# Turned projections: x's hi and lo parts in one 512-column product, copies in eight places, and an addition of halves

## The reference

```python
def first_block(x, ...):
    for l in range(DEPTH):                                   # 2
        x = x + 0.5 * swiglu_ffn(rms_norm(x, ffn1_norm[l]), ffn1_w1[l], ffn1_w2[l])
        h = rms_norm(x, mix_norm[l])
        gm_u, gm_v, r_q, r_k, r_v, r_g, n_q, n_kv, n_g = jnp.split(h @ w_in[l], splits, axis=-1)
        y_a = gmlp_mixer(gelu(gm_u), gelu(gm_v), ...)
        y_b = retention_mixer(r_q, r_k, r_v, r_g, ...)
        y_c = nsa_mixer(n_q, n_kv, n_g, ...)                 # compressed keys, then attention
        g_a, g_b, g_c = jnp.split(sigmoid(h @ w_merge_gate[l] + b_merge_gate[l]), 3, axis=-1)
        mix = g_a * (y_a @ w_branch_out[l, 0]) + g_b * (y_b @ w_branch_out[l, 1]) + g_c * (y_c @ w_branch_out[l, 2])
        x = x + mix @ w_o[l]
        x = x + 0.5 * swiglu_ffn(rms_norm(x, ffn2_norm[l]), ffn2_w1[l], ffn2_w2[l])

def second_block(x, ...):
    for layer in range(DEPTH):                               # 2
        proj = rms_norm_2(x, norm_mix_g[layer]) @ w_in[layer]
        (a_in, bq, bk, bv, cq, ck, cv, co, cgate, dq, dk, dv, gates) = split_cols(proj)
        ys = [fourier_mix(a_in), gqa_branch(bq, bk, bv, ...), mlstm_branch(cq, ck, cv, co, cgate, ...),
              diff_branch(dq, dk, dv, ...)]
        merged = sum(sigmoid(gates[n]) * (ys[n] @ w_branch[layer][n]) for n in range(4))
        x = x + merged @ w_out[layer]
        x = x + conv_ffn(rms_norm_2(x, norm_ffn_g[layer]), ...)
```

## Time and profile before

| | |
|---|---|
| median of 3 runs | 2251.74 us (2251.03 to 2252.18) |
| the profiled execution's own time | 2251.06 us |
| its span in the profile | 2249.3 us |
| instructions | 30453 |
| TensorE matmuls | 12350, busy 2228.1 us |
| VectorE busy | 1532.7 us |
| ScalarE busy | 1209.2 us |
| weight loads | 368 of 1024 KB, median 4.8 us to landing |

### The profile page before, as it was taken

One profiled execution on the slowest core, in us unless ns is written; L12 is line 12 of the kernel. 1 busy time (PEld: TensorE's weight loads), 2 busy tenths in 40 slices (PEclk: granted clock), 3 DMA queues, 4 the chain that ended last, 5 costly groups with the idle time before them and its releaser, 6 DMA issues.

```text
span 2249.3 us, 30453 instructions
## 1 busy us (share of the span) xinstructions
PE 2228.1 (99%) x12350; PEld 1897.9 (84%) x12350; DVE 1532.7 (68%) x2116; ACT 1209.2 (54%) x1808; POOL 65.8 (3%) x118
## 2 busy tenths in 40 slices
PE   8999999999999999999999999999999999999998
PEld 7888987888888889878888888888888888888887
DVE  6567578665665576786566856786777766776766
ACT  6456455554554564555555655455556555455554
POOL 0000000000000000000000100000000100000000
PEclk9999999999999999999999999999999999999999
DMA  8565553455545645434655534444554444445553
GB/s 285 191 231 187 205 183 137 169 189 195 192 175 194 239 176 205 180 138 172 243 187 188 187 132 169 150 159 185 189 188 177 179 150 161 157 162 184 188 187 113
DMA packets 62804, 409.38 MB, mean 182 GB/s; under 512 B 7977, under 2 KB 9513, under 8 KB 15305
## 3 DMA queue, kind: packets, MB, share of 16 engines
q1 hardware_dynamic: 62664, 407.44, 49.8%
HBM read 405.83 MB, written 2.10 MB: 181 GB/s over the span
## 4 chain that ended last, share of the span: by engine, by line
PE 92%; DVE 4%; ACT 2%; DMA 1%; POOL 1%; issue 1%; SPq 0%; POOLq 0%; DVEq 0%; ACTq 0%
PE bank L584 19%; PE bank L585 19%; PE bank L586 19%; PE bank L631 18%; PE bank L638 9%; DVE w_lo L270 2%; DMA w_raw<-in_tiles 1%; PE bank L393 1%; PE bank L1721 1%; PE bank L1733 1%; PE bank L2332 0%; PE bank L1876 0%; PE bank L2500 0%; PE bank L2039 0%; PE bank L2049 0%
## 5 line engine op out<-in xcount | busy, mean ns | idle before, releaser
L270 DVE TENSOR_TENSOR w_lo<-w_raw,w_hi 128x2048 fp32r<-128x2048 f32 x367 | 835.1, 2283 | 56.5 <-ACT w_hi L240 56.1
L240 ACT ACTIVATE w_hi<-w_raw 128x2048 fp32r<-128x2048 f32 x359 | 684.9, 1911 | 107.0 <-DMA w_raw<-in_tiles 106.6
L631 PE MATMUL bank<-hT,w_hi 128*128 128x512 f32 x1920 | 459.7, 391 | 0.7 <-DVE w_lo L270 0.7
L631 PEld LDWEIGHTS bank<-hT,w_hi 128*128 128x128 f32 x1920 | 355.6, 188 | 72.7 <-DVE w_lo L270 1.5
L584 PE MATMUL bank<-w_hi,hT 128*128 128x512 f32 (+2 forms) x832 | 327.5, 394 | 1.3 <-DVE w_lo L223 1.3
L586 PE MATMUL bank<-w_hi,hT 128*128 128x512 f32 (+2 forms) x832 | 318.5, 383 | 0.0
L585 PE MATMUL bank<-w_lo,hT 128*128 128x512 f32 (+2 forms) x832 | 318.3, 383 | 0.0
L638 PEld LDWEIGHTS bank<-hT,w_lo 128*128 128x128 f32 x1920 | 247.7, 191 | 10.3
L638 PE MATMUL bank<-hT,w_lo 128*128 128x256 f32 x1920 | 250.9, 283 | 0.0
L584 PEld LDWEIGHTS bank<-w_hi,hT 128*128 128x128 f32 x832 | 156.6, 188 | 38.2 <-issue 7.8
L586 PEld LDWEIGHTS bank<-w_hi,hT 128*128 128x128 f32 x832 | 156.3, 188 | 31.2
(11 more groups left out here) (395 smaller groups left out, 2987.0 us busy)
## 6 DMA issues: line engine op xcount, KB each, us to landing
w_raw<-in_tiles SPq DMA_DIRECT2D x368, 1024.0 KB, 4.8
a_cmp_w<-in_cmp_w SPq DMA_DIRECT2D x2, 2048.0 KB, 7.7
shifted<-in_bias SPq DMA_DIRECT2D x12, 256.0 KB, 6.6
w_raw<-in_tiles SPq DMA_DIRECT2D x8, 256.0 KB, 5.6
a_gm_rows<-in_rows SPq DMA_DIRECT2D x2, 768.0 KB, 7.1
x_res<-in_x SPq DMA_DIRECT2D x2, 512.0 KB, 5.0
a_ret_rows<-in_rows SPq DMA_DIRECT2D x2, 512.0 KB, 8.3
b_rows<-in_rows SPq DMA_DIRECT2D x2, 512.0 KB, 5.9
```

The lines of the kernel that those rows point to most:

```text
L240: act.activation(k.hi[slot][:], k.raw[slot][:], ACT.Copy).then_inc(k.hi_done[slot], 1)
L270: dve.tensor_tensor(k.lo[slot][:], k.raw[slot][:], k.hi[slot][:].bitcast(F32), ALU.subtract).then_inc(k.lo_done[slot], 1)
L631: pe.matmul(bank[:], k.hi[slot][:, w], k.hT[:, c].rearrange("p a s -> p (a s)"), start=c == 0, stop=False)
```

## The change

A new role `"B"` takes the place of `"T"` for six tiles of block 1 (rqT, rkT, kcvcT, two of nqT, kskwT) and for all ten turned tiles of block 2: 32 tiles over the two layers of each. The two tiles of uT, which go through a Gelu, stay.

For a B unit TensorE runs `both_parts` (8 matmuls of 512 columns) and `lo_part` (8 of 256) into a bank of its own: each unit is now a group, not each tile. ScalarE copies each unit's whole bank (L1141) into one of eight places in the buffers `gate` and `mix`, and VectorE adds the two halves into the output (L1185); a copy waits for the addition eight earlier. `proj_out` of such a tile is now the addition. TensorE signals twice per tile. `Gqa.rope` handles the units of `gqa_a1` before the fold. Waits on other tiles' outputs are added where a mixer begins.

```diff
-            self.units += [(n0, h, h == 1, group, role) for h in range(2)]
-            group += 1
+            apart = role[0] == "B"
+            self.units += [(n0, h, h == 1, group + h * apart, role) for h in range(2)]
+            group += 1 + apart
...
+        self.parts = [a[:].rearrange("p a b -> p (a b)")[:, 2 * SEQ * i:2 * SEQ * (i + 1)] for i in range(4)
+                      for a in (gate, mix)]
...
+            elif role[0] == "B":
+                self.copies += 1
+                key = "act"
+                counts[key] += 1
+                counts["taken"] += 1
+                self.copy_at[u] = self.copies, counts[key]
+                self.proj_out[n] = (self.taken, self.copies)
...
-        first = role[-1] == 0 if role[0] in ("wide", "wgate") else half == 0 or role[0] == "wbranch"
+        first = role[-1] == 0 if role[0] in ("wide", "wgate") else half == 0 or role[0] in ("wbranch", "B")
...
+        elif role[0] == "B":
+            both_parts(pe, k, slot, half, bank)
+            lo_part(pe, k, slot, half, bank).then_inc(k.used[slot], 1)
...
+        if role[0] == "B":
+            copy, _ = self.copy_at[u]
+            k.ring.wait_used(act, n, half + 1)
+            if copy > 8:
+                act.wait_ge(self.taken, copy - 8)
+            act.activation(self.parts[copy % 8], self.bank(group)[:], ACT.Copy, scale=role[1][1]).then_inc(self.act_out, 1)
...
+        if role[0] == "B":
+            copy, at = self.copy_at[u]
+            part = self.parts[copy % 8]
+            dve.wait_ge(self.act_out, at)
+            dve.tensor_tensor(role[2][:, half], part[:, 0:SEQ], part[:, SEQ:2 * SEQ], ALU.add).then_inc(self.taken, 1)
...
         link(last)
+        f.vector(dve, "gqa_a1", lo=False)
         self.fourier.fold(dve)
```

More of the change, by code:

```diff
@@ L39 @@
 WIDE1 = (0, 6, 8, 14)
+BOTH1 = (4, 5, 10, 11, 12, 13)
 F1_AT = 0
@@ L1006, in __init__ @@
         self.tmp = ph.sb("f_tmp", [P, 2, SEQ])
+        self.parts = [a[:].rearrange("p a b -> p (a b)")[:, 2 * SEQ * i:2 * SEQ * (i + 1)] for i in range(4)
+                      for a in (gate, mix)]
+        self.copy_at, self.copies = {}, 0
         self.biased = None if bias is None else ph.sem("f_biased")
@@ L1039, in partial @@
             return role[-1] == 0
-        return not last_half and role[0] != "wbranch"
+        return not last_half and role[0] not in ("wbranch", "B")
     def bank(self, group):
@@ L1117, in activate @@
         n, half, last_half, group, role = self.units[u]
-        if role[0] == "wgate":
+        if role[0] == "B":
[4 more added lines that the diff above has]
+            act.activation(self.parts[copy % 8], self.bank(group)[:], ACT.Copy, scale=role[1][1]).then_inc(self.act_out, 1)
+        elif role[0] == "wgate":
             b, c, kh = role[1:]
+            if kh and not b and self.copies:
+                act.wait_ge(self.taken, self.copies)
             gate = self.gate[:, half, c * 512:(c + 1) * 512]
@@ L1154, in combine @@
         n, half, last_half, group, role = self.units[u]
-        if role[0] == "wgate":
+        if role[0] == "B":
[3 more added lines that the diff above has]
+            dve.tensor_tensor(role[2][:, half], part[:, 0:SEQ], part[:, SEQ:2 * SEQ], ALU.add).then_inc(self.taken, 1)
+        elif role[0] == "wgate":
             b, c, kh = role[1:]
             if kh and self.bias is not None:
+                if not b:
+                    dve.wait_ge(self.taken, self.copies)
                 k.ring.wait_used(dve, n, half + 1)
@@ L2660, in __init__ @@
             ("T", G, uT[:, 0:2], "act"), ("T", G, uT[:, 2:4], "act"),
-            ("T", C, rqT[:], "act"), ("T", C, rkT[:], "act"),
+            ("B", C, rqT[:], "act"), ("B", C, rkT[:], "act"),
             ("wide", C, rv, "act"), ("wide", S, rg, "act"),
-            ("T", C, kcvcT[:], "act"), ("T", Q, nqT[:, 0:2], "act"), ("T", Q, nqT[:, 2:4], "act"),
-            ("T", C, kskwT[:], "act"), ("wide", None, Columns((vsvw, *C), (gates, *T)), "act")],
+            ("B", C, kcvcT[:], "act"), ("B", Q, nqT[:, 0:2], "act"), ("B", Q, nqT[:, 2:4], "act"),
+            ("B", C, kskwT[:], "act"), ("wide", None, Columns((vsvw, *C), (gates, *T)), "act")],
             BRANCHES1, self.bias, gate, mix, ys)
@@ L2731, in __init__ @@
             ("wide", C, qkv[:, :, 0:512], "act"), ("wide", None, Columns((qkv[:, :, 512:768], *C), (g16, *C)), "act"),
[L2732 to L2734 removed]
+            ("B", C, aT[:, 0:2], "act"), ("B", C, aT[:, 2:4], "act"),
+            ("B", C, cqT[:, 0:2], "act"), ("B", C, cqT[:, 2:4], "act"),
+            ("B", C, ckT[:, 0:2], "act"), ("B", C, ckT[:, 2:4], "act"),
             ("wide", C, va[:, :, :, 0:P], "act"), ("wide", T, og, "act"),
[L2736 to L2737 removed]
+            ("B", C, dqT[:, 0:2], "act"), ("B", C, dqT[:, 2:4], "act"),
+            ("B", C, dkT[:, 0:2], "act"), ("B", C, dkT[:, 2:4], "act"),
             ("wide", C, dv, "act")],
@@ L2789, in pool, with middle_signals @@
         self.diff.pool(pool)
-def middle_signals(proj_tiles, wide_at, branches):
-    return [2 if n - 1 in wide_at else 1 for n in range(proj_tiles)] + [2] * (branches * MERGE_TILES) + [1] * (OUT_TILES - 1) + [2]
+def middle_signals(proj_tiles, wide_at, both_at, branches):
+    return [2 if n - 1 in wide_at or n in both_at else 1 for n in range(proj_tiles)] + [2] * (branches * MERGE_TILES) + [1] * (OUT_TILES - 1) + [2]
 def windows(shifted):
@@ L2828, in program @@
             at1.append((ring.add(ffn_places(base + F1_AT), FFN_SIGNALS),
-                        ring.add(list(range(base + PROJ1_AT, base + F2_AT)), middle_signals(PROJ1_TILES, WIDE1, BRANCHES1)),
+                        ring.add(list(range(base + PROJ1_AT, base + F2_AT)), middle_signals(PROJ1_TILES, WIDE1, BOTH1, BRANCHES1)),
                         ring.add(ffn_places(base + F2_AT), END_SIGNALS if l == DEPTH - 1 else FFN_SIGNALS)))
@@ L2832, in program @@
             base = BLOCK2_AT + l * STREAM2
-            at2.append((ring.add(list(range(base + PROJ2_AT, base + UP_AT)), middle_signals(PROJ2_TILES, WIDE2, BRANCHES2)),
+            at2.append((ring.add(list(range(base + PROJ2_AT, base + UP_AT)), middle_signals(PROJ2_TILES, WIDE2, BOTH2, BRANCHES2)),
                         ring.add(ffn_places(base + UP_AT), END_SIGNALS if l == DEPTH - 1 else FFN_SIGNALS)))
```

4 lines of the change are left out of this document (added).

## The result

| | before | changed |
|---|---|---|
| median | 2251.47 us (20 runs, 2248.96 to 2253.12) | 2256.60 us (20 runs, 2253.53 to 2258.52) |
| the profiled execution's own time | 2251.06 us | 2257.90 us |
| its span | 2249.3 us | 2256.2 us |

The ratio is 1.0021, 95% interval 1.0015 to 1.0027. The change costs 5.1 us, 0.23%: slower, as forecast, but by less than half of the +11.8 us of the sum. The two profiled executions lie 6.84 us apart, since the one of the changed kernel is among its slower ones; terms are compared with this 6.84.

A forecast was written before the change was run, and what follows sets the result against it. TensorE, busy 2228.1 of 2249.3 us, was taken to bound the kernel. Merging -7.0, nqT waits +4.9 and +3.2, rv +1.0, Fourier +4.7, clock +5.0 gave +11.8, so 2263.5 us; range 2255.5 to 2269.5.

The forecast's parts named there:

- the sum: Whole kernel: savings of merging plus new waits and clock falls, +11.8 us, giving 2263.5 us; chance 0.55.
- merging, 32 tiles: Turned projections of both blocks: 16 of 48 matmuls go, saving 0.22 us a tile, -7.0 us.
- wait at nqT: Block 1: third nqT unit waits for ScalarE's first copy, behind tile 14's conversion; 4.9 us layer 1, 3.2 layer 2.
- rv's first matmul: Block 1: it waits for ScalarE's copy of rkT's first unit, delayed behind VectorE's work; 0.5 us per layer, +1.0.
- Fourier stretch: Block 2, before the Fourier copy: four VectorE additions cost 1.45 us, four tiles' savings lost; 2.33 per layer, +4.7.
- clock: Behind the longer waits in blocks 1 and 2: three more falls to 1.2 GHz, +5.0 us; bounds none and twice that.
- the fixed cost of a matmul: TensorE: the skill's about 2.5 ns per matmul would give back 1.3 us for 512; the prediction took 12 ns from rows.
- merging buys nothing: Turned projections: fewer matmuls give no gain, so the 7.0 us are gone; from rows +17.0, 2268.7 us; chance 0.03.
- What costs nothing: Elsewhere: extra ScalarE copies (19 us), VectorE additions (27 us), signals and added waits don't delay TensorE; 0 us.
- the late one named there: Block 1: VectorE's retention chain comes 1.8 us later, covered by the nqT wait; without that, some 1.3 us.
- the rival in which the waits come and the clock doesn't fall more: Both blocks: the new waits appear without further clock falls; +6.8 us, 2258.5 us; chance 0.22 for waits with fewer falls.

The follow-up runs named there:

- The two experiments on GpSimd: pool_free_before and pool_held_after, which move VectorE's `w_lo` away from or back beside GpSimd's root operation in block 2: 2252.78 and 2262.30 us.
- pool_free_before: Kernel before, with block 2's VectorE `w_lo` beside GpSimd's root moved behind the scaling of the heads: 2252.78 us, ratio 1.0002.
- pool_held_after: Changed kernel, with that block 2 `w_lo` put ahead of aT's first two additions, beside GpSimd's root again: 2262.30 us, ratio 1.0043.
- best: Changed kernel, tile 14's load before kcvcT's transfers, block 1's `w_lo` before additions, block 2's `w_lo` behind Fourier copies: 2240.97 us, ratio 0.9950.
- before_fm: Kernel before, with only block 2's `w_lo` in front of the Fourier copies made behind them: 2244.85 us, ratio 0.9970.

## Why the prediction was right or wrong

The sum, term by term, for the two profiled executions (+6.84 us):

| term | forecast | measured |
|---|---|---|
| merging, 32 tiles | -7.0 | -5.4 |
| wait at nqT | +8.1 | +6.0 |
| rv's first matmul | +1.0 | +1.1 |
| Fourier stretch | +4.7 | +0.6 |
| clock | +5.0 | +4.4 |
| start of the kernel, not the change's | 0 | +0.3 |
| sum | +11.8 | +7.0 |

Merging is 32 tiles by 0.17 us (below); the Fourier stretch is what was lost of the savings of its eight tiles (8 x 0.17, of which 0.43 + 0.31 were seen). 0.2 us of the sum are too much. The medians lie 5.1 us apart, 1.7 less, which is as much as one fall of the clock costs.

- **The step that failed** is the one on the Fourier copy: "Together 2.33 for each layer, +4.7. The wait in the trace grows from 2.5 to about 4.8 us." The four additions did cost what I said: from the start of the scaling to the end of the copies it takes 15.58 us before and 17.05 after. But I took that start as fixed against TensorE. It came 1.9 us earlier, at 10.8 instead of 12.7 us behind aT's first matmul, because GpSimd's operation in front of it fell from 2.19 to 0.32 us. Its row wasn't among those that I read; I stopped at "[3.84 <-POOL b_gqa_rs L166]" of the earlier trace rows and did not ask what those 3.84 us and the ones before were made of. The two experiments on GpSimd show this cause, and it accounts for 3.7 of the 4.8 us between the sums. What is left is the wait at nqT, 2.1 us too large, and merging, 1.6 too large the other way; that these nearly cancel is luck. The Trainium skill (SBUF — State Buffer, SBUF: two separate sides) has the rule: a VectorE operation with two SBUF inputs and a GpSimd operation that reads SBUF share a pair of ports, and whoever starts first keeps the other out for its whole instruction. The rows of GpSimd's operation in before, changed, pool_free_before and pool_held_after agree (2.19, 0.32, 0.29, 2.18 us); the other direction of the rule did not show (last section).
- **The wait at nqT**: mechanism, place and chain were right, the size in layer 1 too large, 4.9 against 3.1 us. The load took 4.7 us from SyncE's issue to ScalarE's start, where it had taken 6.2, so that the bank was free at 275.1 and not at 276.3; and TensorE was done with the tile at 272.2, where I had 271.4. In layer 2, with 5.0 us for the same load, the forecast 3.2 stands against 2.9.
- **Merging** was priced with one feed-forward tile of 5.54 us. That tile stands behind 512-column matmuls. A unit that stands behind 256-column ones steps at 2.79 us, 5.59 for a tile, and at 2.89 behind a mixer's small products, so a tile saves some 0.17 and not 0.22. The units of nqT in best show both (starts 265.41, 268.30, 271.09, 273.88):

```profile
265.41 2.09 PE L633 MATMUL bank<-hT,w_hi 128*128 128x512 f32 x8
267.34 1.12 PE L640 MATMUL bank<-hT,w_lo 128*128 128x256 f32 x8
268.30 2.00 PE L633 MATMUL bank<-hT,w_hi 128*128 128x512 f32 x8
270.14 1.11 PE L640 MATMUL bank<-hT,w_lo 128*128 128x256 f32 x8
271.09 2.00 PE L633 MATMUL bank<-hT,w_hi 128*128 128x512 f32 x8
```

  The same holds of the fixed cost of a matmul that the prediction weighed: 16 fewer matmuls for each tile gave back 0.17/16 = 11 ns apiece (9 by the 0.14 of best), far above the 2.5 ns that the Trainium skill gives (TensorE: Matmul & The Clock Gate, Wait — 56ns, not 53.3ns?), from which 1.3 us would have come. The rival "merging buys nothing" falls: best gains 3.6 us more than before_fm.
- **rv's first matmul** came as forecast, at two places of 0.57 us each (idle 0.3 in the wait's row).
- **The clock** came out near the forecast in the profiled execution, 4.4 against 5.0, but not by the falls that I counted: there are two more than before, one of them twice as long. Both waits at nqT have one, and of the two Fourier waits still one. It is a matter of chance from run to run, see below; the median run has fewer than the profiled one.
- **What costs nothing** held, and so did the late one named there: the retention's chain, "some 1.3 us", measured 1.5 to 1.8 once the wait before it was gone. That it was worth a fix of its own I had not seen.

The sign was right for the right reason, block 1; the size was wrong by a term in block 2 that never came. The measured 2256.6 us lies at the low end of the range, 1.9 under the rival in which the waits come and the clock doesn't fall more; that is luck, since the clock did fall and what was missing is the Fourier term.

## What to carry to other kernels

A form that doubles the outputs of a product makes every order written for single outputs suspect: look at what stands between two outputs on the copying engine (here a conversion behind a late load), on the adding engine (a `w_lo` behind the last addition), and on the queue that feeds both. Before pricing work that is added to a chain, ask what the chain's start waits for, down to the smallest engine; whatever moves there moves all of it. And a kernel that is 0.2% slower may hold a form that is faster: two changes of order made +5 us into -6.

## What the runs showed of the hardware

- **GpSimd beside VectorE.** An operation of GpSimd on 20 columns took 0.29 us alone, 0.31 to 0.39 when a VectorE addition of 0.42 us had begun 0.17 to 0.25 us earlier, and 2.18 to 2.26 when a `w_lo` of 2.28 us had; both are VectorE operations with two SBUF inputs, and GpSimd's ended 0.14 to 0.15 us behind theirs each time. The other direction did not show: GpSimd's next operation (3.57 us, two inputs, begun 0.03 us earlier) ran beside a whole `w_lo` in the changed kernel; it took 3.57 us as always, and the `w_lo` 2.34 against a mean of 2.28. By the rule of the Trainium skill (SBUF — State Buffer, SBUF: two separate sides) the `w_lo` would have been kept out for the rest of the 3.57 us; the measurement decides, and says no for this pair of operations.
- **The clock after an idle time.** In nine profiles with waits of this size (before, changed and seven experiments) TensorE started no matmul for 2.65 to 2.8 us at 13 places, and at three of them the granted clock fell to 1.2 GHz for 3.4 us; with 2.9 to 3.4 us it fell at seven places of nine, once for 6.8 us; with 4.5 us at both, once for 6.8 us; with 2.1 us or less, within the layers, at none. The falls began between 2.3 us before and 1.4 us after the end of the idle time. The 20 runs of the changed kernel go with their mean granted clock, on average 2253.7 us at 0.999, 2255.1 at 0.998, 2257.0 at 0.997, 2257.9 at 0.996. Where no such wait is left, the spread shrinks: best ran from 2240.49 to 2241.31 us, the kernel before from 2249.09 to 2253.22 beside it.
